# Gate and up weights of sixteen experts in one 16 KB-run transfer, down weights in 8 KB runs: one layer step on one Trainium2 core

## The chip, the cores and the metric

The kernel runs as one program on one core of a Trainium2 chip. Its time is the device time of one execution in microseconds (us); several executions are timed and the median is given. One further execution is profiled, which records every instruction, wait and DMA packet.

## The reference, cut to what matters

One decoder layer is computed for 1024 new prompt tokens and 8 sequences of 8 sampled tokens (1088 tokens of width 1024): a norm, one q/k/v projection, two kinds of attention (partly over cached pages), an output projection, and a mixture of 16 experts of which every token takes two. Only the experts matter here:

```python
# 4 groups x 4 experts; w_gate, w_up: (.., 1024, 256); w_down: (.., 256, 1024); all float32
a = silu(einsum('nd,gedf->ngef', xt, w_gate)) * einsum('nd,gedf->ngef', xt, w_up)
y = einsum('ngef,gefd->nd', a * gates[..., None], w_down)     # gates: two of 16 are not zero
x = x + y
```

Gate, up and down weights take 1 MB each for an expert, 3 MB in all.

## The kernel before

The stages run one after the other: projection, attention, output projection, `route`, `experts`. `route` (L2043) picks two experts for each token and sorts the tokens by expert into tiles of 128 rows: 32 tile slots (`MOE_TILES`), of which an expert fills as many as it needs. Which expert a tile belongs to is known only on the chip, so `tile_expert`, `tile_load` and `tile_place` are tables in memory that the engines read into registers (L2374, L2385, L2386).

`experts` (L2310) walks over the 32 tiles. For a tile the engines do this:

- SyncE (SP) issues the weight loads. Every tile has three transfers, each with a condition (`cond=load`): gate and up (L2395), down (L2400). A transfer whose condition is 0 moves nothing, but raises its semaphore like one that ran. A tile's expert is loaded only in the first tile of that expert. There are four places for weights (`W_PLACES`). The gate and up transfers of a tile wait until the tile four before it has been split (`gu_lo`); the down transfer waits until the down product of the tile four before is in PSUM (`y_done`). As the SP's queue goes in order, the next tile's gate and up transfers come right behind that wait. The weights of experts 0 and 1 are loaded ahead in `route` by `load_ahead` (L2028), with three transfers each and without a condition, and the SP waits for those of a tile before it goes on (L2389).
- ScalarE (ACT) and VectorE (DVE) split gate and up weights into a high and a low part (L2574, L2516), in two halves of 128 x 2048 elements. ACT's split waits for `gu_loaded` (L2567).
- TensorE (PE) multiplies the rows with the split weights, 24 matmuls (`gate_up`, L2467), turns the next tile's rows round (L2445), makes the down product of the tile before (`down`, L2489), and turns the activations round (L2476). Tile 0 is multiplied with whole weights, 16 matmuls (L2457).
- ACT and DVE copy the two halves of the down product out of PSUM (`keep_y`, L2605, L2539). Both wait for the addition two tiles back, since `expert_out` has two buffers.
- GpSimd (POOL) gathers the rows of the tile (L2038) and adds the result rows to the residual in memory with an indirect, accumulating DMA (L2423). Each addition waits until the one before it has landed. Gathers and additions go through the software DMA queue q0; all that SP issues goes through the hardware queue q1. Both run on the same 16 DMA engines.

A transfer from DRAM is moved as runs that are contiguous on both sides. Partition p of the gate weights holds rows 8p to 8p+7, each of 256 numbers: one run of 8 KB. Partition p of the down weights holds rows p and 128+p, each of 1024 numbers: two runs of 4 KB.

After the last addition the SP loads the residual rows back, they are normed, and stored.

Of the kernel before, what the change touches and what calls it, by code (L numbers as in the profile page):

```python
# [10 lines left out]
F32 = mybir.dt.float32  # L11
# [21 lines left out]
P = 128  # L33
# [1965 lines left out]
def expert_places(nc, ctx, t):  # L1999

    def keep(name, shape, dt=F32):
        return ctx.enter_context(nc.sbuf_tensor(name, shape, dt))

    t.slot_gate = keep("slot_gate", [P, MOE_TILES])
    t.slot_tok = keep("slot_tok", [P, MOE_TILES], I32)
    t.slot_out = keep("slot_out", [P, MOE_TILES], I32)
    t.adds_wanted = keep("adds_wanted", [1, 1], I32)
    t.tile_expert = keep("tile_expert", [1, MOE_TILES], I32)
    t.tile_load = keep("tile_load", [1, MOE_TILES], I32)
    t.tile_place = keep("tile_place", [1, MOE_TILES], I32)  # L2010
    t.w_gu = keep("w_gate_up", [P, W_PLACES, 2, KC, D_EXPERT])
    t.w_dn = keep("w_down", [P, W_PLACES, FK, D_MODEL])
    t.slot_rows = keep("slot_rows", [P, ROW_PLACES, D_MODEL])
    assert place_ahead(N_EXPERTS - 1) == 0
    freed = t.w_gu[:, 1:W_PLACES, :, :, :].rearrange("p a c k n -> p (a c k n)").rearrange("p (t n) -> p t n", n=D_MODEL)
    t.x1_rows, t.g_final_row, t.square3 = freed[:, 0:TILES, :], freed[:, TILES, :], freed[:, TILES + 1, :]
    t.x1_loaded = [ctx.enter_context(nc.semaphore(f"x1_loaded{n}")) for n in range(TILES)]
    t.g_final_loaded = ctx.enter_context(nc.semaphore("g_final_loaded"))
    t.w_ahead = [ctx.enter_context(nc.semaphore(f"expert_ahead{n}")) for n in range(W_AHEAD)]
    t.added = ctx.enter_context(nc.semaphore("expert_rows_added"))  # L2020
    t.rows_loaded = [ctx.enter_context(nc.semaphore(f"slot_rows_loaded{n}")) for n in range(ROW_PLACES)]
# [6 lines left out]
def load_ahead(engine, t, e):  # L2028


    n = place_ahead(e)
    for c, w in enumerate((t.w_gate, t.w_up)):
        engine.dma_start(t.w_gu[:, n, c, :, :], w[e].rearrange("(p k) n -> p k n", p=P)).then_inc(t.w_ahead[e], 16)
    engine.dma_start(t.w_dn[:, n, :, :], t.w_down[e].rearrange("(k p) n -> p k n", p=P)).then_inc(t.w_ahead[e], 16)

# [274 lines left out]
def experts(nc, t):  # L2310

    with ExitStack() as ctx:
# [67 lines left out]
        with nc.Block() as block:  # L2380

            @block.sync
            def _(sp):
                for tile in range(MOE_TILES):
                    e = sp.value_load(t.tile_expert[0:1, tile:tile + 1], min_val=0, max_val=N_EXPERTS - 1)  # L2385
                    load = sp.value_load(t.tile_load[0:1, tile:tile + 1], min_val=0, max_val=1)  # L2386
                    at = place(sp, tile)
                    if tile < W_AHEAD:
                        sp.wait_ge(t.w_ahead[tile], 48)  # L2389
                    gu_lo.reached(sp, tile - W_PLACES, 1)  # L2390
                    if tile == W_PLACES:
                        gu_done.reached(sp, 0)
                    own_wait(sp, t)
                    for n, w in enumerate((t.w_gate, t.w_up)):
                        sp.dma_start(w_gu[:, bass.ds(at, 1), n, :, :].rearrange("p a k n -> p (a k) n"),  # L2395
                                     w[bass.ds(e, 1), :, :].rearrange("e (p k) n -> p (e k) n", p=P),
                                     cond=load).then_inc(gu_loaded[tile % W_PLACES], 16)
                    y_done.reached(sp, tile - W_PLACES, 1)
                    own_wait(sp, t)
                    sp.dma_start(w_dn[:, bass.ds(at, 1), :, :].rearrange("p a k n -> p (a k) n"),  # L2400
                                 t.w_down[bass.ds(e, 1), :, :].rearrange("e (k p) n -> p (e k) n", p=P),
                                 cond=load).then_inc(dn_loaded[tile % W_PLACES], 16)
# [36 lines left out]
            def _(pe):  # L2439
# [10 lines left out]
                def gate_up(tile):  # L2450
                    u = tile % 2
                    if tile == 0:
                        pe.wait_ge(t.w_ahead[0], 48)
                        for k in range(KC):
                            if k % 4 == 0:
                                xT_hi.reached(pe, 0, k // 4)
                            last = pe.matmul(gu_ps[:, 0, :].rearrange("p (c n) -> p c n", c=2), whole_T[:, k, :],  # L2457
                                             w_gu[:, place_ahead(0), :, k, :], start=(k == 0), stop=(k == KC - 1))
                        last.then_inc(gu_done.sem, 1)
                        return  # L2460
# [18 lines left out]
                def down(tile, halves=(0, 1)):  # L2479
# [3 lines left out]
                    if tile < W_AHEAD:  # L2483
                        pe.wait_ge(t.w_ahead[tile], 48)
                    for c in halves:
# [22 lines left out]
            def _(dve):  # L2508
                def split_gu(tile):

                    raw = w_gu[:, bass.ds(place(dve, tile), 1), :, :, :].rearrange("p a c k n -> p k (a c) n")
                    for half in range(2):
                        at, u = slice(4 * half, 4 * half + 4), tile % 2
                        gu_hi.reached(dve, tile, half)
                        own_wait(dve, t)
                        dve.tensor_tensor(gu_split[:, u, 1, at, :].rearrange("p k (c n) -> p k c n", c=2), raw[:, at, :, :],  # L2516
                                          gu_split[:, u, 0, at, :].bitcast(F32).rearrange("p k (c n) -> p k c n", c=2),
                                          ALU.subtract).then_inc(gu_lo.sem, 1)
# [44 lines left out]
            def _(act):  # L2563
                def split_gu(tile):

                    raw = w_gu[:, bass.ds(place(act, tile), 1), :, :, :].rearrange("p a c k n -> p k (a c) n")
                    act.wait_ge(gu_loaded[tile % W_PLACES], 32 * (tile // W_PLACES) + 32)  # L2567
                    if tile < W_AHEAD:
                        act.wait_ge(t.w_ahead[tile], 48)
                    gu_done.reached(act, tile - 2)  # L2570
                    own_wait(act, t)
                    for half in range(2):
                        at, u = slice(4 * half, 4 * half + 4), tile % 2
                        act.activation(gu_split[:, u, 0, at, :].rearrange("p k (c n) -> p k c n", c=2), raw[:, at, :, :],  # L2574
                                       ACT.Copy).then_inc(gu_hi.sem, 1)

# [73 lines left out]
def host_constants():  # L2650
# [26 lines left out]
INPUTS = ["x", "cache_kT_d", "cache_v_d", "cache_kT_s", "cache_v_s", "page_table", "rel_bias", "g_mix", "w_in", "lambda_q1", "lambda_k1", "lambda_q2",  # L2677
          "lambda_k2", "subln_g", "w_out", "g_ffn", "w_group", "b_group", "w_erouter", "b_erouter", "w_gate", "w_up",
          "w_down", "g_final", "eye", "bucket_table", "mask_rows", "half_map", "rank_const", "column_const", "spare_const", "before_const", "token_const", "sum_map"]
# [96 lines left out]
```

## Time and profile before

| | |
|---|---|
| median of 3 timed executions | 1261.24 us (1259.09 to 1262.69) |
| the profiled execution, its own time | 1258.88 us |
| its span, first to last instruction | 1256.9 us |
| mean granted TensorE clock | 0.971 of full speed |
| PE busy in the span | 1156.9 us (92%) |
| DVE, ACT, POOL busy | 698.2, 597.1, 142.5 us |
| route and experts | from 875 us to the end |

The profile gives for each engine when it was busy, what ended each wait, and for each DMA queue how many packets and bytes moved in a stretch of time. 2 us of the profiled execution's time lie outside its span. The busy share of PE is an average over all stages; what the change is worth has to be read from the expert stage alone.

### The profile page before, as it was taken

Reading aid. Unit: us, or ns where it says so; the run is one execution under the profiler, and the core shown is the slowest. Engines: PE = TensorE matmul, PEld = TensorE weight load, DVE = VectorE, ACT = ScalarE, POOL = GpSimd, SP = SyncE. Lnnn points to the kernel's source line nnn. Section 1 sums busy time; section 2 is a strip of 40 time slices with the busy share of each in tenths; the row PEclk is TensorE's granted clock in tenths of the full one; section 3 lists DMA queues with packets and bytes.
Section 4 is the critical chain, followed back from the end, with each engine's and each line's share of the span. In section 5 each row is a group of like instructions: output and inputs, shape, how many; then the busy total and the mean of one; then the engine's idle time right before and its main releaser. Section 6 shows DMA issues by size and latency. Waiting matters only on the chain. (4 is left out here: it accounts for less than half of the span.)

```text
span 1256.9 us, 23325 instructions
## 1 busy us (share of the span) xinstructions
PE 1156.9 (92%) x7695; PEld 815.2 (65%) x7695; DVE 698.2 (56%) x1048; ACT 597.1 (48%) x1030; POOL 142.5 (11%) x172
## 2 busy tenths in 40 slices
PE   7999999999688999979999999997689999999992
PEld 5877888888445555544655567875367766667771
DVE  4322112220177776658899977444566666666664
ACT  5520122201176776737568554232155655556654
POOL 1100000000011111100000000000123222433311
PEclk9999999999899999989999999999689999999997
DMA  6642244317599999999999946442679999865476
GB/s 209 218 132 77 82 148 126 101 42 250 189 360 381 345 374 386 382 380 379 383 362 371 387 159 185 155 147 107 245 274 363 375 378 297 239 171 112 101 218 193
DMA packets 155392, 307.43 MB, mean 245 GB/s; under 512 B 22311, under 2 KB 49354, under 8 KB 151178
## 3 DMA queue, kind: packets, MB, share of 16 engines
q1 hardware_dynamic: 145018, 272.38, 60.0%
q0 software_dynamic: 9216, 33.56, 11.5%
q8 instruction: 64, 1.05, 0.3%
q14 instruction: 54, 0.44, 0.1%
q10 hardware_dynamic: 1040, 0.00, 0.0%
HBM read 308.31 MB, written 54.72 MB: 289 GB/s over the span
## 5 line engine op out<-in xcount | busy, mean ns | idle before, releaser
L327 PE MATMUL proj_ps<-w_in_split,x_T_hi 128*128 128x512 f32 x608 | 194.6, 395 | 2.7 <-DVE w_in_split L369 2.7
L2516 DVE TENSOR_TENSOR w_gate_up_split<-w_gate_up,w_gate_up_split 128x2048 fp32r<-128x2048 f32 x62 | 139.3, 2288 | 87.3 <-ACT w_gate_up_split L2574 87.3
L2467 PE MATMUL gate_up_ps<-w_gate_up_split,slot_rows_T 128*128 128x512 f32 x744 | 180.3, 398 | 2.1 <-DVE slot_rows_T L2524 1.9
L2467 PEld LDWEIGHTS gate_up_ps<-w_gate_up_split,slot_rows_T 128*128 128x128 f32 x744 | 139.2, 191 | 31.9 <-DVE slot_rows_T L2524 3.4
L327 PEld LDWEIGHTS proj_ps<-w_in_split,x_T_hi 128*128 128x128 f32 x608 | 115.0, 189 | 27.8 <-DVE x_T_lo L364 2.5
L455 ACT ACTIVATE proj_rows<-proj_ps,sum_squares 128x512 f32<-128x512 f32 x38 | 26.2, 689 | 211.9 <-PE proj_ps L327 200.3
L327 PE MATMUL proj_ps<-w_in_split,x_T_lo 128*128 128x512 f32 x304 | 119.1, 392 | 0.0
L2574 ACT ACTIVATE w_gate_up_split<-w_gate_up 128x2048 fp32r x62 | 115.3, 1912 | 6.7 <-DMA w_gate_up<-in_w_up 5.4
L2489 PE MATMUL expert_out_ps<-w_down,expert_act_T 128*128 x256 | 115.3, 593 | 0.3 <-issue 0.3
L1736 PE MATMUL mix_out_ps<-w_out_split,oT_split 128*128 128x512 f32 x420 | 101.2, 396 | 0.3 <-DVE w_out_split L1875 0.3
L1142 PE MATMUL turns_and_scores_ps<-head_kT,head_qT 64*128 64x512 f32 (+3 forms) x384 | 85.9, 537 | 16.2 <-DMA head_kT<-scratch_kT 9.9
L1736 PEld LDWEIGHTS mix_out_ps<-w_out_split,oT_split 128*128 128x128 f32 x420 | 77.6, 188 | 18.9 <-DVE w_out_split L1875 1.8
L1317 DVE TENSOR_TENSOR_SCAN rest_products<-rest_products 128x128 f32<-128x128 f32 (+7 forms) x64 | 84.2, 1342 | 3.4 <-ACT rest_products L1478 3.4
L322 PE MATMUL proj_ps<-x_T_hi,w_in_split 128*128 128x512 f32 x256 | 82.3, 396 | 0.0
L1506 ACT ACTIVATE weights_T<-turns_and_scores_ps 128x1024 f32<-128x1024 f32 (+6 forms) x80 | 58.8, 742 | 42.1 <-PE turns_and_scores_ps L1156 41.6
L2423 POOL DMA_INDIRECT scratch_x<-expert_out,slot_out x32 | 58.2, 1818 | 179.5 <-DMA scratch_x<-expert_out,slot_out 95.2
L2489 PEld LDWEIGHTS expert_out_ps<-w_down,expert_act_T 128*128 128x128 f32 x256 | 46.2, 190 | 46.5 <-issue 46.4
L1240 PE MATMUL sample_o_ps<-pages,sample_weights_T 128*32 128x256 f32 x1024 | 71.1, 385 | 0.4 <-ACT sample_weights_T L1557 0.4
L369 DVE SCALAR_TENSOR_TENSOR w_in_split<-w_in_now,g_mix_T,w_in_split 128x512 fp32r<-128x512 f32 x48 | 35.6, 748 | 58.8 <-ACT w_in_split L441 58.8
L1206 PE MATMUL turns_and_scores_ps<-pages,q_by_block 128*32 128x256 f32 x912 | 61.2, 391 | 5.1 <-ACT betas L1482 3.4
L327 PEld LDWEIGHTS proj_ps<-w_in_split,x_T_lo 128*128 128x128 f32 x304 | 57.6, 189 | 11.3
L1118 POOL TENSOR_SCALAR stats<-stats 128x1 f32<-128x1 f32 x32 | 8.9, 279 | 445.4 <-ACT o_squares L1516 445.4
(255 smaller groups left out, 1750.1 us busy)
## 6 DMA issues: line engine op xcount, KB each, us to landing
w_gate_up<-in_w_gate SPq DMA_DIRECT2D x34, 1024.0 KB, 8.4
w_gate_up<-in_w_up SPq DMA_DIRECT2D x34, 1024.0 KB, 10.2
w_down<-in_w_down SPq DMA_DIRECT2D x34, 1024.0 KB, 12.3
pages<-in_cache_v_d SPq DMA_DIRECT2D x128, 256.0 KB, 5.9
pages<-in_cache_kT_s SPq DMA_DIRECT2D x128, 256.0 KB, 5.7
pages<-in_cache_v_s SPq DMA_DIRECT2D x128, 256.0 KB, 6.0
pages<-in_cache_kT_d SPq DMA_DIRECT2D x100, 256.0 KB, 6.2
w_in_now<-in_w_in SPq DMA_DIRECT2D x48, 256.0 KB, 3.0
```

What stands on the lines that cost most here:

```text
L322: last = pe.matmul(pj_ps[:, n % PJ_BANKS, 0:c1 - c0], w[g % 2][:, k, at], h[:, k, c0:c1], start=(k == 0 and m == 0), stop=(k == KC - 1 and ...
L327: last = pe.matmul(pj_ps[:, n % PJ_BANKS, :], h[:, k, at], w[g % 2][:, k, :], start=(k == 0 and m == 0), stop=(k == KC - 1 and m == 2))
L1142: last = pe.matmul(ring[places["score", it, i, g]][:, u, 0:k1 - k0], qT[half(u), it % 2, i * P:(i + 1) * P], kT[half(u), it % 2, k0:k1], s ...
L1206: last = pe.matmul(out, q_block[:, e, b, :], keys, start=(part == 0), stop=(part == 1))
L1240: last = pe.matmul(sO_ps[rows, :], sT[0:n, s, rows], page_v[0:n, c // 2, b:b + 2, :], start=(s == 0), stop=(s == D_PAGES - 1))
L1317: dve.tensor_tensor_scan(x, x, x, 1.0, ALU.mult, ALU.bypass).then_inc(scans.sem, 1)
L1506: act.activation(wT[:, at:at + m, :], blocks_of("out", it, i, n)[:, 0:m, :], ACT.Copy)\
L1736: last = pe.matmul(y_ps[:, m % Y_BANKS, :], oT_split[:, n % 2, a, k, :], w_split[:, b, k, c * BANK:(c + 1) * BANK], start=(m > 0 and at == ...
L2467: last = pe.matmul(gu_ps[:, u, :], xT[:, u, a, k, :], gu_split[:, u, b, k, :], start=(k == 0 and m == 0), stop=(k == KC - 1 and m == 2))
L2489: last = pe.matmul(y_ps[:, c, :], aT[:, u, k, :], w_dn[:, bass.ds(at, 1), k, c * BANK:(c + 1) * BANK] .rearrange("p a n -> p (a n)"), star ...
L2516: dve.tensor_tensor(gu_split[:, u, 1, at, :].rearrange("p k (c n) -> p k c n", c=2), raw[:, at, :, :], gu_split[:, u, 0, at, :].bitcast(F3 ...
L2574: act.activation(gu_split[:, u, 0, at, :].rearrange("p k (c n) -> p k c n", c=2), raw[:, at, :, :], ACT.Copy).then_inc(gu_hi.sem, 1)
```

## The change

The host packs gate and up weights of an expert side by side (`w_gate_up`, 1024 rows of 512 numbers), and reorders the down weights so that partition p holds two neighbouring rows. In memory on the chip, the tile `w_gate_up` has the same size as before, with gate and up of one row of the weights side by side. So a transfer of gate and up is one of 2 MB with one contiguous run of 16 KB for each partition, in place of two of 1 MB with runs of 8 KB. The down transfer stays at 1 MB, with one run of 8 KB for each partition in place of two of 4 KB. The bytes are the same. Each tile has two conditional transfers in place of three, and an expert loaded ahead has two in place of three. The operands of the splits and of tile 0's matmuls become contiguous where they were two pieces of 256 for each k; their number and sizes stay. Counts that are waited for become smaller with the number of transfers.

```diff
-    t.w_gu = keep("w_gate_up", [P, W_PLACES, 2, KC, D_EXPERT])
+    t.w_gu = keep("w_gate_up", [P, W_PLACES, KC, GU])
...
-    for c, w in enumerate((t.w_gate, t.w_up)):
-        engine.dma_start(t.w_gu[:, n, c, :, :], w[e].rearrange("(p k) n -> p k n", p=P)).then_inc(t.w_ahead[e], 16)
-    engine.dma_start(t.w_dn[:, n, :, :], t.w_down[e].rearrange("(k p) n -> p k n", p=P)).then_inc(t.w_ahead[e], 16)
+    engine.dma_start(t.w_gu[:, n, :, :], t.w_gate_up[e].rearrange("(p k) n -> p k n", p=P)).then_inc(t.w_ahead[e], 16)
+    engine.dma_start(t.w_dn[:, n, :, :], t.w_down[e].rearrange("(p k) n -> p k n", p=P)).then_inc(t.w_ahead[e], 16)
...
-                        sp.wait_ge(t.w_ahead[tile], 48)
+                        sp.wait_ge(t.w_ahead[tile], 32)
...
-                    for n, w in enumerate((t.w_gate, t.w_up)):
-                        sp.dma_start(w_gu[:, bass.ds(at, 1), n, :, :].rearrange("p a k n -> p (a k) n"),
-                                     w[bass.ds(e, 1), :, :].rearrange("e (p k) n -> p (e k) n", p=P),
-                                     cond=load).then_inc(gu_loaded[tile % W_PLACES], 16)
+                    sp.dma_start(w_gu[:, bass.ds(at, 1), :, :].rearrange("p a k n -> p (a k) n"),
+                                 t.w_gate_up[bass.ds(e, 1), :, :].rearrange("e (p k) n -> p (e k) n", p=P),
+                                 cond=load).then_inc(gu_loaded[tile % W_PLACES], 16)
...
-                                 t.w_down[bass.ds(e, 1), :, :].rearrange("e (k p) n -> p (e k) n", p=P),
+                                 t.w_down[bass.ds(e, 1), :, :].rearrange("e (p k) n -> p (e k) n", p=P),
...
-                            last = pe.matmul(gu_ps[:, 0, :].rearrange("p (c n) -> p c n", c=2), whole_T[:, k, :],
-                                             w_gu[:, place_ahead(0), :, k, :], start=(k == 0), stop=(k == KC - 1))
+                            last = pe.matmul(gu_ps[:, 0, :], whole_T[:, k, :],
+                                             w_gu[:, place_ahead(0), k, :], start=(k == 0), stop=(k == KC - 1))
...
-                        dve.tensor_tensor(gu_split[:, u, 1, at, :].rearrange("p k (c n) -> p k c n", c=2), raw[:, at, :, :],
-                                          gu_split[:, u, 0, at, :].bitcast(F32).rearrange("p k (c n) -> p k c n", c=2),
+                        dve.tensor_tensor(gu_split[:, u, 1, at, :], raw[:, at, :], gu_split[:, u, 0, at, :].bitcast(F32),
                                           ALU.subtract).then_inc(gu_lo.sem, 1)
...
-                    act.wait_ge(gu_loaded[tile % W_PLACES], 32 * (tile // W_PLACES) + 32)
+                    act.wait_ge(gu_loaded[tile % W_PLACES], 16 * (tile // W_PLACES) + 16)
...
-                        act.activation(gu_split[:, u, 0, at, :].rearrange("p k (c n) -> p k c n", c=2), raw[:, at, :, :],
-                                       ACT.Copy).then_inc(gu_hi.sem, 1)
+                        act.activation(gu_split[:, u, 0, at, :], raw[:, at, :], ACT.Copy).then_inc(gu_hi.sem, 1)
...
-    for name in ("w_gate", "w_up"):
-        host[name] = a[name][0].reshape(N_EXPERTS, D_MODEL, D_EXPERT)
-    host["w_down"] = a["w_down"][0].reshape(N_EXPERTS, D_EXPERT, D_MODEL)
+    host["w_gate_up"] = np.concatenate([a[name][0].reshape(N_EXPERTS, D_MODEL, D_EXPERT) for name in ("w_gate", "w_up")], axis=2)
+    host["w_down"] = a["w_down"][0].reshape(N_EXPERTS, FK, P, D_MODEL).transpose(0, 2, 1, 3).reshape(N_EXPERTS, D_EXPERT, D_MODEL)
```

## Rows read from the trace of the kernel before

**Rows 1.** One window: busy us of PE, PEld, DVE, ACT, POOL, clock, DMA share, GB/s

```profile
1000.00:1050.00 50.00, 49.11 (x203) 33.52 (x201) 32.40 (x28) 28.65 (x33) 10.39 (x9) 1.00 1.03 371
```

**Rows 2.** Chain that ended last, start of the expert stage: start us, us, what

```profile
906.88 0.06 DMA w_gate_up<-in_w_up
...
907.15 1.92 ACT w_gate_up_split L2574
...
911.52 2.29 DVE w_gate_up_split L2516
...
915.39 8.31 PE gate_up_ps L2467 x24
...
928.23 5.49 PE gate_up_ps L2467 x24
```

**Rows 3.** SP's own queue in order of time: start us, us, transfer issued

```profile
902.86 0.00 SPq L2395 DMA_DIRECT2D w_gate_up<-in_w_gate  x1
903.59 0.01 SPq L2395 DMA_DIRECT2D w_gate_up<-in_w_up  x1
...
906.59 0.08 SPq L2395 DMA_DIRECT2D w_gate_up<-in_w_gate  x1
...
1018.38 0.39 SPq L2400 DMA_DIRECT2D w_down<-in_w_down  x1
1021.17 0.11 SPq L2395 DMA_DIRECT2D w_gate_up<-in_w_gate  x1
```

**Rows 4.** The same chain, later: additions, then TensorE again

```profile
938.57 0.68 ACT expert_out L2605
...
939.59 11.37 DMA scratch_x<-expert_out,slot_out
...
1042.07 10.03 DMA scratch_x<-expert_out,slot_out
...
1052.18 0.29 ACT expert_out L2605
...
1071.42 5.48 PE gate_up_ps L2467 x24
...
1221.62 5.49 PE gate_up_ps L2467 x24
```

**Rows 5.** Waits from 1000 to 1075 us: total us, times, longest

```profile
ACT expert_out L2605 <- DMA scratch_x<-expert_out,slot_out: 5.8, 4, 2.2
```

**Rows 6.** DMA queues in 952:954, 985:987, 991:994, 1028:1032, 1052:1057: packets, MB, share

```profile
q1 hardware_dynamic: 209, 0.86, 103.8%
...
q1 hardware_dynamic: 101, 0.41, 50.2%
q0 software_dynamic: 102, 0.41, 49.7%
...
q0 software_dynamic: 79, 0.32, 53.8%
q1 hardware_dynamic: 78, 0.61, 50.7%
...
q1 hardware_dynamic: 195, 0.83, 51.1%
...
q1 hardware_dynamic: 287, 1.12, 54.6%
```

**Rows 7.** All 32 additions (L2423), issue to landing

```profile
DMA to landing us min/median/max: 5.8/7.2/11.4
```

**Rows 8.** Groups of instructions: split halves and a four times smaller subtraction

```profile
L2516 DVE TENSOR_TENSOR w_gate_up_split<-w_gate_up,w_gate_up_split 128x2048 fp32r<-128x2048 f32 x62 | 139.3, 2288 | 87.3 <-ACT w_gate_up_split L2574 87.3
...
L2524 DVE TENSOR_TENSOR slot_rows_T<-slot_rows_T_ps,slot_rows_T 128x512 fp32r<-128x512 f32 x62 | 39.6, 680 | 0.2 <-ACT slot_rows_T L2583 0.2
```

**Rows 9.** Windows of 1 us, columns as in rows 1

```profile
914.00:915.00 1.00, 0.69 (x2) 0.29 (x2) 1.00 (x3) 0.08 (x1) 0.00 (x0) 0.53 0.94 365
...
920.00:921.00 1.00, 1.00 (x4) 0.78 (x3) 1.00 (x2) 0.00 (x0) 0.00 (x0) 0.55 0.99 406
```

More of the change, by code:

```diff
@@ L2014, in expert_places @@
     assert place_ahead(N_EXPERTS - 1) == 0
-    freed = t.w_gu[:, 1:W_PLACES, :, :, :].rearrange("p a c k n -> p (a c k n)").rearrange("p (t n) -> p t n", n=D_MODEL)
+    freed = t.w_gu[:, 1:W_PLACES, :, :].rearrange("p a k n -> p (a k n)").rearrange("p (t n) -> p t n", n=D_MODEL)
     t.x1_rows, t.g_final_row, t.square3 = freed[:, 0:TILES, :], freed[:, TILES, :], freed[:, TILES + 1, :]
@@ L2452, in gate_up @@
                     if tile == 0:
-                        pe.wait_ge(t.w_ahead[0], 48)
+                        pe.wait_ge(t.w_ahead[0], 32)
                         for k in range(KC):
@@ L2483, in down @@
                     if tile < W_AHEAD:
-                        pe.wait_ge(t.w_ahead[tile], 48)
+                        pe.wait_ge(t.w_ahead[tile], 32)
                     for c in halves:
@@ L2509, in split_gu @@
                 def split_gu(tile):
-                    raw = w_gu[:, bass.ds(place(dve, tile), 1), :, :, :].rearrange("p a c k n -> p k (a c) n")
+                    raw = w_gu[:, bass.ds(place(dve, tile), 1), :, :].rearrange("p a k n -> p (a k) n")
                     for half in range(2):
@@ L2564, in split_gu @@
                 def split_gu(tile):
-                    raw = w_gu[:, bass.ds(place(act, tile), 1), :, :, :].rearrange("p a c k n -> p k (a c) n")
-                    act.wait_ge(gu_loaded[tile % W_PLACES], 32 * (tile // W_PLACES) + 32)
+                    raw = w_gu[:, bass.ds(place(act, tile), 1), :, :].rearrange("p a k n -> p (a k) n")
+                    act.wait_ge(gu_loaded[tile % W_PLACES], 16 * (tile // W_PLACES) + 16)
                     if tile < W_AHEAD:
-                        act.wait_ge(t.w_ahead[tile], 48)
+                        act.wait_ge(t.w_ahead[tile], 32)
                     gu_done.reached(act, tile - 2)
@@ L2677 @@
 INPUTS = ["x", "cache_kT_d", "cache_v_d", "cache_kT_s", "cache_v_s", "page_table", "rel_bias", "g_mix", "w_in", "lambda_q1", "lambda_k1", "lambda_q2",
-          "lambda_k2", "subln_g", "w_out", "g_ffn", "w_group", "b_group", "w_erouter", "b_erouter", "w_gate", "w_up",
+          "lambda_k2", "subln_g", "w_out", "g_ffn", "w_group", "b_group", "w_erouter", "b_erouter", "w_gate_up",
           "w_down", "g_final", "eye", "bucket_table", "mask_rows", "half_map", "rank_const", "column_const", "spare_const", "before_const", "token_const", "sum_map"]
```

## The prediction

> **What bounds the kernel now.** I first read the page for the shares, and then only the expert stage, since the change touches nothing else. The window view shows PE busy for 49.11 of 50 us while the DMA engines are at a share of 1.03 [rows 1]: two resources are full at once. The chain that ended last says which one sets the end. It enters the stage through SP's queue: an SP transfer ends a wait, ACT splits tile 1's weights, DVE subtracts and copies rows, and PE starts tile 1 at 915.39 [rows 2]. From 928.23 on a tile should take (1221.62 - 1071.42) / 15 = 10.01 us, the pace of an unstalled PE [rows 4]. From 928.23 to 1071.42 lie 14 tiles, 140.2 us at that pace, but 143.2 us passed [rows 2, 4]. So PE loses 3.0 us to waits in the stretch in which weights are loaded, and nothing after it. The chain says to whom: it runs through additions, the first issued at 939.59, the last at 1042.07 [rows 4]. These are ten, each of which waits for the one before; from 939.59 to the landing of the last, 1052.10, they take 11.25 us each against PE's 10.01. ACT's copy of the down product waits for them four times, 5.8 us together, 2.2 at the longest [rows 5]. An addition lands 5.8 us after its issue at the least and 11.4 us at the most [rows 7]: the weight loads make it late.
>
> The packets show how. In 952:954 q1 alone moves 0.43 MB/us, in packets of 4.1 KB. In 985:987 both queues are busy and move 101 and 102 packets, all of 4 KB. In 991:994 they move 78 and 79, but those of q1 have 8 KB: 0.61 MB against 0.32 [rows 6]. The engines take one packet from one queue, then one from the other, whatever its length. The packet is the contiguous run, and the run is what the change doubles.
>
> **The change part by part.**
>
> *One conditional transfer fewer, start of the stage.* ACT's split of tile 1 starts 0.27 us after SP's up transfer of tile 1 at 906.88 [rows 2]. That transfer moves nothing (expert 1 was loaded ahead), but its semaphore ends the wait; so SP's queue is the path. On it lie tile 0's gate and up transfers, 903.59 - 902.86 = 0.73 us apart, and tile 1's, 906.88 - 906.59 = 0.29 us apart [rows 2, 3]. One of each goes: 1.0 us. All that follows to 915.39 (ACT, DVE, DVE) is work without slack, so tile 1 starts 1.0 us earlier, and with it SP's loads and the first addition. The bounds: 0.3 us, if the 0.73 is a stall that moves to the next transfer, and 1.3 us. I take 1.0. In the steady stage SP waits for `y_done` for most of a tile, and its removed transfer is worth nothing: that wait hides it. Without that cover it would be 0.3 to 0.7 us a tile.
>
> *The splits and tile 0's matmuls.* Their operands become contiguous. The subtraction takes 2288 ns for 2048 elements in four times two pieces, a smaller one 680 ns for 512: 1608 / 1536 = 1.05 ns an element and 0.14 us at the start, with nothing left for the pieces [rows 8]. Nothing gained, between 0 and the 0.14 us of one start a half, hidden by PE.
>
> *Load bytes and rates.* The bytes stay. 4 KB packets alone already run at 0.43 MB/us (0.86 MB in 2 us) [rows 6]. The nearest figure for longer ones is the mixed window's 0.61 MB in 1.5 us of q1's share, 0.40. I take no gain and no loss. The bounds: at 0.40 in place of 0.43 an expert's 3.1 MB take 0.5 us more, 5 us of engine time over ten experts; in the other direction, no more than PE's 3.0 us of stall can vanish.
>
> *The run length in front of the additions.* Of an addition's 128 rows each of 16 engines moves 8, one packet each. With gate and up runs queued, each waits for one of q1's packets: 8 KB at 0.43 MB/us over 16 engines is 0.31 us, 16 KB is 0.61 us. Eight of them cost 2.4 us more for each addition. Against down runs it is 8 x (0.31 - 0.15) = 1.2 us more. But q1 can go ahead only with what is queued. In 1028:1032 it still moves 4 KB runs, that is down weights issued at 1018.38, with gate and up of 1021.17 behind them [rows 3, 6]: up to 3 MB, 7 us of loads, could pass an addition there. At the last critical addition, landing at 1052.10, what q1 has left is the 1.12 MB of 1052:1057, 2.6 us [rows 6]. So an addition around 1030 gets later by 0 to 7 us, the one at 1052.10 by 0 to 2.6. What is served early is not served later, so the additions catch up. PE's stall follows the addition that is latest against PE's pace. The copy that waits for the one at 1052.10 comes 11 tiles after the copy at 938.57 [rows 4], so at 10.01 us a tile it is due at 1048.7: 3.4 us behind. The addition two before (about 1030, due 1028.7) is 1.3 behind. With 2.0 us more at the last it is 5.4 behind; with 4 us more at 1030 that one is 5.3 behind, which comes to the same. I take 2.0, near the upper end of 2.6, since in the nearest row, the one of 8 KB, double length did take double bytes. So the stall grows by +2.0; bounds 0 and +5 (7 us more at 1030, 8.3 behind in place of 3.4).
>
> *The other rule.* The Trainium skill (DMA: Bandwidth & Descriptors, Queues, rings and completion order) says that an engine drains a whole packet, typically 9 to 17 descriptors, from one ring before it switches. The rows show one recorded packet against one. By that rule the additions would wait for 9 to 17 runs at each switch and not for one: 8 x 9 x 0.31 us, 22 us an addition before the change, where the longest landing is 11.4 in all. So its packet isn't a row's packet here, and the sum goes by the row.
>
> **Sum.** -1.0 + 0 + 0 + 2.0 = +1.0 us on the profiled execution: its span 1256.9 and the 2.0 around it, 1258.88, become 1259.9. The median of the runs shown, 1261.24, lies 2.4 above it; the same difference gives 1262.2.
>
> **The rivals.**
>
> *The clock stays up.* PE stands still before tile 1, and its granted clock is 0.53 of full in 914:915 and 0.55 in 920:921, the low level (1.2 GHz) from about 914.1 to 920.9 [rows 9]. Tile 1's 24 matmuls take 8.31 us, tile 2's 5.49 [rows 2]: the low level costs 2.8 us. PE's next work came in the same window (busy 0.69 us of it). With work there 1.0 us sooner the clock may not fall: 1262.2 - 2.8 = 1259.4. Against it: most of the standstill stays.
>
> *Run length doesn't matter.* If the new transfer is cut into the same packets as before, or the queue holds too little to pass the additions, only the first part remains: 1261.2 - 1.0 = 1260.2. For it: the rows show no packet above 8 KB. Against: both lengths there are one run each.
>
> *Additions become the bound (the other side).* Before, an addition lands 10.0 us after its issue under load [rows 4] and 5.8 without [rows 7]: q1 is in front of it for 4.2 of the 7.3 us that an expert's 3.1 MB take at 0.43 MB/us, and the rest passes in the addition's idle parts (descriptors made, end signalled). With longer runs q1 empties its queue in front of the addition, and then the engines stand idle in those parts. If it is 5.0 us in place of 4.2, ten additions get 8 us later, and no catching up follows, since the loads are paced by PE, which waits as well: +8 - 1 = +7, 1268. It decides once q1 runs dry between additions. For it: the doubled bytes in 991:994. Against: nine tiles in a row load an expert each, so that the queue is long.
>
> *Faster engines.* The 3.0 us of stall vanish with the 1.0: 1257.2, or less with the clock.
>
> **How the numbers follow.** Forecast 0.35 (its own range 1259.5 to 1265), clock up 0.2, run length without effect 0.15, additions as the bound 0.22, faster engines 0.08. A measurement of this kernel tells a change from none at about 0.3%, 3.8 us: 1257.5 and 1265.0. Faster: the 0.08 and half of the clock case, which reaches below 1257.5 where the additions don't get later, 0.18. Slower: 0.22 and the forecast's tail, 0.25. Within: 0.57. The range 1257 to 1268 leaves out about 0.1 on each side.
>
> **What would show it.** SP's first transfer for tile 1 at about 905.9 and PE's tile 1 at 914.4. Packets of 16 KB in q1, one against one of q0, with 0.1 MB of q0 for 0.4 of q1. Additions that land 11 to 13 us after issue from 975 to 1030, in place of 10 to 11, and then catch up; ACT's waits for them at 8 us in place of 5.8; gate and up weights landing earlier. I am wrong if q1's packets stay at 8 KB, if additions land no later, or if tile 1's matmuls run at the full clock.

## The result

| | before | after | ratio, 95% interval |
|---|---|---|---|
| median of 15 timed executions each, side by side | 1260.4 us | 1266.69 us | 1.0049 [1.0038, 1.0059] |
| the same, once more (28 and 12 executions) | 1260.38 us | 1264.79 us | 1.0040 [1.0026, 1.0054] |
| span of the profiled execution | 1256.9 us | 1265.2 us | |

The changed kernel is slower, by 4 to 6 us. The forecast was 1262.2, with 1257 to 1268 as the range. So the range holds the result, but the estimate is 4.5 us short: 1266.7 lies above the 1259.5 to 1265 that the forecast had as its own range, in the part that the prediction called slower (0.25), and nearest to the rival of 1268. The second comparison, 4.4 us above the kernel before, is at the upper edge of the forecast's own range.

The start of the stage in the chain that ended last, after the change (start us, us, what):

```profile
909.46 0.06 DMA w_gate_up<-in_w_gate_up
...
909.74 1.92 ACT w_gate_up_split L2571
...
914.10 2.28 DVE w_gate_up_split L2514
```

It is the path of [rows 2], step by step, with SP's single transfer where its second one was. Before the 8.3 us of longer span are put down to the change, it has to be seen where the stage begins. Below is the router's first operation in DVE's timeline: of before, of after, and of a second profile of each (experiments e8 and e9 below):

```profile
875.04 0.19 DVE L2134 TENSOR_REDUCE g_max<-logits 128x9 f32<-128x36 f32 x1 [0.32 <-PEq L1669]
```
```profile
879.06 0.19 DVE L2133 TENSOR_REDUCE g_max<-logits 128x9 f32<-128x36 f32 x1 [0.32 <-PEq L1669]
```
```profile
878.82 0.19 DVE L2134 TENSOR_REDUCE g_max<-logits 128x9 f32<-128x36 f32 x1 [0.33 <-PEq L1669]
```
```profile
875.64 0.19 DVE L2133 TENSOR_REDUCE g_max<-logits 128x9 f32<-128x36 f32 x1 [0.33 <-PEq L1669]
```

Each kernel has an early and a late one. So 4.0 of the 8.3 us belong to the execution and not to the change, and from here on everything is counted from this operation. It leaves 1256.9 - 875.04 = 381.9 us before and 1265.2 - 879.06 = 386.1 us after.

This is tile 1 in TensorE's timeline, of after and of the second profile of before:

```profile
917.97 7.25 PE L2465 MATMUL gate_up_ps<-w_gate_up_split,slot_rows_T 128*128 128x512 f32 x24 [0.75 <-DVE slot_rows_T L2521]
```
```profile
918.02 5.78 PE L2467 MATMUL gate_up_ps<-w_gate_up_split,slot_rows_T 128*128 128x512 f32 x24 [0.76 <-DVE slot_rows_T L2524]
```

And its clock after, two windows of 1 us with the columns of [rows 1]:

```profile
914.00:915.00 1.00, 0.89 (x9) 0.66 (x6) 1.00 (x2) 0.99 (x2) 0.00 (x0) 1.00 0.00 0
...
918.00:919.00 1.00, 1.00 (x3) 0.81 (x4) 0.00 (x0) 1.00 (x1) 0.00 (x0) 0.50 1.11 475
```

The granted clock is full at 914, and at the low level (0.50, 1.2 GHz) at 918, after PE had stood still for most of 915 to 918. Compared with [rows 9], the clock still falls, but stays low for a shorter time (3.4 us against 6.8).

Then the additions, further on in the chain that ended last:

```profile
990.97 11.96 DMA scratch_x<-expert_out,slot_out
...
1003.72 12.52 DMA scratch_x<-expert_out,slot_out
...
1017.03 12.35 DMA scratch_x<-expert_out,slot_out
...
1029.46 0.30 ACT expert_out L2601
...
1038.44 5.78 PE gate_up_ps L2465 x24
...
1229.80 5.49 PE gate_up_ps L2465 x24
```

The additions of the same numbers before the change, in its chain:

```profile
986.27 10.25 DMA scratch_x<-expert_out,slot_out
...
997.31 10.19 DMA scratch_x<-expert_out,slot_out
...
1008.29 10.82 DMA scratch_x<-expert_out,slot_out
```

Three in a row take 12.0 to 12.5 us in place of 10.2 to 10.8. The last of them lands at 1029.38 against 1019.11, though the addition with the number of the first one in [rows 4] had started only 1.9 us later than before (941.5 against 939.6). While this lasts, PE starts a tile every 12.4, 13.3 and 13.1 us (999.6, 1012.0, 1025.3, 1038.4). PE's lost time is counted from the start of tile 2, 929.50, to that of the last tile, 29 tiles later, at 1229.55, which is 300.05 us. At the unstalled pace (150.20 / 15 = 10.013 us a tile) it would be 290.4, so 9.7 us are lost, against 3.0 before. The waits from 985 to 1075 us, to be compared with [rows 5]:

```profile
DVE expert_out L2536 <- DMA scratch_x<-expert_out,slot_out: 15.2, 5, 4.4
ACT expert_out L2601 <- DMA scratch_x<-expert_out,slot_out: 13.4, 4, 4.7
```

ACT's 5.8 us have become 13.4. The queues after, in 985:987, 1012:1014 and 1042:1054:

```profile
q1 hardware_dynamic: 52, 0.43, 52.6%
q0 software_dynamic: 50, 0.20, 49.1%
...
q1 hardware_dynamic: 36, 0.59, 70.3%
q0 software_dynamic: 32, 0.13, 32.7%
...
q0 software_dynamic: 525, 1.95, 79.1%
q1 hardware_dynamic: 6, 0.02, 0.5%
```

In the first window q1's packets have 8 KB (the down weights now, which were the 4 KB of [rows 6]), in the second 16 KB, and they alternate with q0's nearly one for one. What passes an addition between its issue and its landing has grown with it. These are q1's packets and bytes in that time, for one addition before (1008.29:1019.11) and for two after (1003.72:1016.24 and 1017.03:1029.38):

```profile
q1 hardware_dynamic: 525, 3.00, 67.6%
...
q1 hardware_dynamic: 354, 3.71, 70.5%
...
q1 hardware_dynamic: 338, 3.55, 68.4%
```

Before, it is about the 3.1 MB of one expert; after, it is 0.6 to 0.7 MB more, 1.3 to 1.7 us at the 0.43 MB/us of [rows 6].

From 1042 to 1054, q1 moves next to nothing. The weights are not done by then: another expert's 3.15 MB come from 1054 to 1068. But SP may issue them only when PE has finished the down product of an earlier tile, and PE is late. These are q1 in 1054:1068, and SP's wait in 1010:1060:

```profile
q1 hardware_dynamic: 288, 3.15, 60.9%
```
```profile
SPq L86 <- PE expert_out_ps L2487: 34.5, 4, 10.2
```

Last, the windows of both resources after, columns as in [rows 1]:

```profile
980.00:1005.00 25.00, 25.00 (x108) 18.14 (x107) 13.94 (x13) 14.49 (x17) 4.82 (x4) 1.00 1.02 380
1005.00:1030.00 25.00, 20.26 (x83) 13.36 (x82) 13.32 (x12) 10.67 (x14) 3.83 (x4) 1.00 1.03 383
1030.00:1042.00 12.00, 9.35 (x38) 6.00 (x37) 7.00 (x7) 7.82 (x9) 4.13 (x3) 1.00 0.96 354
1042.00:1054.00 12.00, 12.00 (x52) 8.61 (x51) 8.99 (x8) 8.12 (x9) 3.54 (x3) 1.00 0.80 166
```

The DMA engines are full (1.03) just where PE misses 4.7 of 25 us. They do not work less, they work in another order: from 940 to 1042 q1 moves 28.29 MB after and 27.63 MB before, although tile 2 began 1.5 us later. The weights were ahead, and the additions paid for it.

### The profile page after: what moved, and what is told of

Read it like the earlier page. It is cut to its first block and busy times, and to the rows that moved or that the text cites. A ratio compares the mean times of both kernels' runs of the same rounds, so it can differ in the third digit from the quotient of the medians.

```text
span 1265.2 us, 23259 instructions
## 1 busy us (share of the span) xinstructions
PE 1156.3 (91%) x7695; PEld 814.2 (64%) x7695; DVE 698.4 (55%) x1048; ACT 597.8 (47%) x1030; POOL 149.1 (12%) x172
## 3 DMA queue, kind: packets, MB, share of 16 engines
q1 hardware_dynamic: 140666, 272.38, 59.7%
q0 software_dynamic: 9216, 33.56, 11.5%
## 5 line engine op out<-in xcount | busy, mean ns | idle before, releaser
L2514 DVE TENSOR_TENSOR w_gate_up_split<-w_gate_up,w_gate_up_split 128x2048 fp32r<-128x2048 f32 x62 | 139.3, 2288 | 86.6 <-ACT w_gate_up_split L2571 86.6
L1142 PE MATMUL turns_and_scores_ps<-head_kT,head_qT 64*128 64x512 f32 (+3 forms) x384 | 85.8, 537 | 20.4 <-DMA head_kT<-scratch_kT 10.1
L2421 POOL DMA_INDIRECT scratch_x<-expert_out,slot_out x32 | 65.8, 2056 | 189.4 <-DMA scratch_x<-expert_out,slot_out 95.9
L327 PEld LDWEIGHTS proj_ps<-w_in_split,x_T_lo 128*128 128x128 f32 x304 | 57.6, 189 | 11.3
```

What stands on the lines that cost most here:

```text
L327: last = pe.matmul(pj_ps[:, n % PJ_BANKS, :], h[:, k, at], w[g % 2][:, k, :], start=(k == 0 and m == 0), stop=(k == KC - 1 and m == 2))
L1142: last = pe.matmul(ring[places["score", it, i, g]][:, u, 0:k1 - k0], qT[half(u), it % 2, i * P:(i + 1) * P], kT[half(u), it % 2, k0:k1], s ...
L2421: pool.indirect_dma_start(t.x1[:, :], bass.IndirectOffsetOnAxis(ap=t.slot_out[:, tile:tile + 1], axis=0), y[:, tile % 2, :], None, compute ...
L2514: dve.tensor_tensor(gu_split[:, u, 1, at, :], raw[:, at, :], gu_split[:, u, 0, at, :].bitcast(F32), ALU.subtract).then_inc(gu_lo.sem, 1)
```

## The experiments

All but e8, which is one profile, are timed beside the kernel before on the same chip. "Places for y" is the number of buffers for the down product. "Lost" is PE's lost time as above; "start" is from the router's first operation to tile 1.

| | gate and up | down | places for y | ratio, 95% interval | lost us | start us | tile 1 us |
|---|---|---|---|---|---|---|---|
| before, first profile | 2 transfers, 8 KB | 4 KB | 2 | 1 | 3.0 | 40.35 | 8.31 |
| e8, before again | 2 transfers, 8 KB | 4 KB | 2 | | 3.8 | 39.20 | 5.78 |
| after | 1, 16 KB | 8 KB | 2 | 1.0049 [1.0038, 1.0059] | 9.7 | 38.91 | 7.25 |
| e9, after again | 1, 16 KB | 8 KB | 2 | 1.0040 [1.0026, 1.0054] | 9.3 | 38.67 | 7.33 |
| e1 | 1, 16 KB | 4 KB | 2 | 1.0001 [0.9988, 1.0015] | 5.5 | 38.85 | 5.75 |
| e2 | 2, 8 KB | 8 KB | 2 | 1.002 [1.0004, 1.0035] | 4.2 | 39.29 | 8.62 |
| e3 | 1, two of 8 KB | 4 KB | 2 | 0.9986 [0.9973, 0.9998] | 4.9 | 38.86 | 5.75 |
| e4 | 1, four of 4 KB | 4 KB | 2 | 1.0017 [1.0003, 1.003] | 5.3 | 38.88 | 5.74 |
| e5 | 1, 16 KB | 8 KB | 3 | 0.9998 [0.9986, 1.0011] | 0.7 | 38.73 | 7.21 |
| e6 | 2, 8 KB | 4 KB | 3 | 0.9991 [0.9976, 1.0006] | 2.8 | 39.23 | 7.06 |
| e7 | 1, two of 8 KB | 4 KB | 3 | 0.998 [0.9966, 0.9994] | 3.1 | 38.83 | 5.74 |
| e11, e7 again | 1, two of 8 KB | 4 KB | 3 | 0.9983 [0.9967, 0.9998] | 4.0 | 38.94 | 5.74 |
| e10 | 1, 16 KB | 4 KB | 3 | 0.9969 [0.9955, 0.9982] | 0.1 | 38.78 | 5.76 |

**e1: the changed kernel with down weights in 4 KB runs again.**

```diff
-    engine.dma_start(t.w_dn[:, n, :, :], t.w_down[e].rearrange("(p k) n -> p k n", p=P)).then_inc(t.w_ahead[e], 16)
+    engine.dma_start(t.w_dn[:, n, :, :], t.w_down[e].rearrange("(k p) n -> p k n", p=P)).then_inc(t.w_ahead[e], 16)
```

(and the same in SP's conditional transfer and on the host)

> Gate and up as in the change (one transfer, runs of 16 KB), down weights with 4 KB runs as before. Theory (each packet of the weight queue goes in front of one packet of an addition, so run length sets how late additions land): additions against gate and up wait as in the changed kernel, additions against down weights as before, so most of the loss stays: 1.002 to 1.005 of before; additions land 11 to 12.5 us after issue between 980 and 1040 us. Rival (the loss comes from the down weights, or from something outside the expert stage): 0.998 to 1.001.

1261.67 us beside 1261.43. I had expected most of the loss to stay, since 16 KB runs are the longer ones, and it is gone. Its queues in 1005:1007 and 1012:1014:

```profile
q0 software_dynamic: 67, 0.27, 68.5%
q1 hardware_dynamic: 62, 0.25, 33.1%
...
q1 hardware_dynamic: 55, 0.84, 99.0%
q0 software_dynamic: 1, 0.00, 0.0%
```

In the first window an addition passes and meets the down weights, 4 KB against 4 KB. In the second the 16 KB runs have the engines for themselves, since q0 is between two of its transfers. This is not a matter of one window. Below are e1's addition before this one, in 1001:1004 (q1 alone, 16 KB) and 1004:1010, and the changed kernel in 1009:1014:

```profile
q1 hardware_dynamic: 83, 1.31, 101.6%
...
q0 software_dynamic: 220, 0.84, 56.3%
q1 hardware_dynamic: 221, 1.05, 44.0%
...
q1 hardware_dynamic: 94, 1.49, 71.2%
q0 software_dynamic: 85, 0.35, 34.7%
```

An addition gets late by what it meets. In e1 the additions around here meet mostly the short runs and land 10.4 to 11.0 us after issue; in the changed kernel they meet the long ones and land after 12.0 to 12.5.

**e2: the kernel before, with down weights in 8 KB runs.** The same edit the other way.

> Gate and up as before (two transfers, 8 KB runs), only the down weights with 8 KB runs. Theory: 1.2 us more for an addition that meets down weights, none for one that meets gate and up, and no gain at the start: 1.000 to 1.003 of before. Rival (run length doesn't matter): 1.000.

1263.56 us, 1.002. The ratio is as expected, the reason is not: the seven additions issued from 979 to 1046 land after 10.1 to 10.8 us, before after 9.7 to 10.8, so the expected 1.2 us more are not there. PE loses 4.2 us against 3.0 and 3.8, and tile 1 took 8.62 us in this profile. So 8 KB down runs alone are worth about +2 us, of which the profile gives 0.4 to 1.2 to waits after tile 2, and neither half of the change alone makes the whole loss. Together they do: e1 less e3, 16 KB in place of 8 KB, is +0.0015, e2 less before +0.002, both together less e3 +0.0054 to 0.0063. With intervals of 0.0013 to each side of a ratio that alone would not be firm, but the lost times say it too: 3.0 and 3.8 before, 4.2 and 5.5 with one of them, 9.7 and 9.3 with both. With both lengths doubled there is no short run left for an addition to meet.

**e3: one transfer for gate and up, in two runs of 8 KB for each partition; down 4 KB.** The change without its longer runs; the edit is against the changed kernel.

```diff
+GU_RUNS = 2
...
-                    sp.dma_start(w_gu[:, bass.ds(at, 1), :, :].rearrange("p a k n -> p (a k) n"),
-                                 t.w_gate_up[bass.ds(e, 1), :, :].rearrange("e (p k) n -> p (e k) n", p=P),
+                    sp.dma_start(w_gu[:, bass.ds(at, 1), :, :].rearrange("p a (h k) n -> p (a h) (k n)", h=GU_RUNS),
+                                 t.w_gate_up[bass.ds(e, 1), :, :].rearrange("e (h p k) n -> p (e h) (k n)", h=GU_RUNS, p=P),
```

> One transfer for gate and up, but the host lays the weights out so that each partition gets two runs of 8 KB; down weights with 4 KB runs as before. So only the number of transfers differs from before. Theory: tile 1 starts 1.0 to 1.6 us earlier and additions land as before: 0.998 to 0.9995. Rival (the packing itself, or one large transfer, is what makes it slower): 1.003 or more.

1259.31 us, 0.9986. The merged transfer, the side by side layout and the contiguous operands cost nothing; if anything they give 2 us. The ratio is in the expected range, though the start gained 0.3 to 0.4 us on e8 and e2 and not 1.0 to 1.6. The loss is in the run lengths.

**e4: the same with four runs of 4 KB (`GU_RUNS = 4`).**

> As the run before this one, but four runs of 4 KB a partition for gate and up. Theory: an addition waits for 4 KB where it waited for 8, 8 x 0.15 = 1.2 us less for each against gate and up; additions land after 9 us, TensorE's stall of 3.0 us goes, and the start gains 1.0 to 1.6: 0.996 to 0.998. Rival (short runs are slower to move, weights come late): 1.000 or more, with ACT's split waiting for weights.

1263.13 us, 1.0017, where 0.996 to 0.998 was expected: the rival's way. The additions are earlier, 9.1 to 10.8 us from 985 to 1049, and ACT and DVE don't wait for one from 985 to 1075. But ACT waits for gate and up weights there, and the chain runs through one of these transfers:

```profile
ACT w_gate_up_split L2573 <- DMA w_gate_up<-in_w_gate_up: 10.4, 5, 2.9
```
```profile
1020.16 23.53 DMA w_gate_up<-in_w_gate_up
```

So the run length moves the wait from one queue to the other: 4 KB makes the weights late, 16 and 8 KB together the additions, and the 8 and 4 KB of before lie between the two.

**e5: the changed kernel with three places for the down product.** Gate and activations share one buffer, which makes the room. The lengths of all runs and the work stay.

```diff
-                    if tile >= 2:
-                        act.wait_ge(t.added, 16 * (tile - 1))
-                    act.activation(y[:, u, 0:BANK], y_ps[:, 0, :], ACT.Copy, scale=t.slot_gate[:, tile:tile + 1])\
+                    if tile >= Y_PLACES:
+                        act.wait_ge(t.added, 16 * (tile - Y_PLACES + 1))
+                    act.activation(y[:, tile % Y_PLACES, 0:BANK], y_ps[:, 0, :], ACT.Copy, scale=t.slot_gate[:, tile:tile + 1])\
```

(with `Y_PLACES = 3`; the same in DVE's half and in the addition; `silu_gate` has one place, is multiplied in place, and ACT waits for `aT_done` of the tile before)

> The changed kernel with three buffers for the expert outputs in place of two, so that ACT and VectorE copy a down product without waiting for the addition two tiles back, but three back (room comes from one buffer for the activations in place of four). Theory (TensorE's 9.7 us of lost time come from additions that land late): the third buffer gives each addition 10 us more, so 7 to 9.7 us of them go: 0.996 to 0.999 of the kernel before the change. Rival (weights or another wait is behind it): no gain, 1.004.

1258.94 us beside 1259.76; the changed kernel has 1266.69 and 1264.79 beside 1260.4. The additions issued from 979 to 1026 land after 10.3 to 13.0 us, two of the five after more than 11, but from 985 to 1075 only POOL waits for one:

```profile
POOL scratch_x L2421 <- DMA scratch_x<-expert_out,slot_out: 53.5, 7, 10.4
```

PE's loss falls from 9.7 to 0.7 us. This is the most direct evidence for the cause: with the same run lengths, and ACT and DVE no longer behind the additions, PE does not stall. The time fell less than the loss, by 5 to 7 us against 9, so that 0.9998 lies just above what was expected (0.996 to 0.999); where the rest went is not shown.

**e6: the kernel before with three places.**

> The kernel before the change with the same three buffers. Theory: its 3.0 us of lost time go, 0.997 to 0.998 of the kernel before. Rival (with the additions out of the way the weights come late, as they are at the edge too): 0.998 to 1.001.

1259.8 us, 0.9991: level with before, as the rival had it (0.998 to 1.001). The waits for additions are gone here too, and in their place ACT waits for weights, 940 to 1130 us:

```profile
ACT w_gate_up_split L2573 <- DMA w_gate_up<-in_w_up: 5.8, 3, 2.8
```

With one limit taken away, PE still loses 2.8 us to the other, against 3.0 and 3.8 with both: the two limits of the kernel before lie side by side.

**e7: e3 with three places.**

> One transfer for gate and up with two runs of 8 KB a partition, down weights with 4 KB runs, and three buffers for the expert outputs. Theory: the start gains 1.5 us and up to 2.6 from a clock that stays up at tile 1, and the 4.9 us that TensorE lost in the same kernel with two buffers go: 0.993 to 0.996. Rival (the weights are the next bound): 0.996 to 0.999, with ACT's split waiting for weights.

1257.36 us, 0.998, where 0.993 to 0.996 was expected; again the rival. Weights are the limit as in e6 (5.2 us of ACT's wait, longest 2.9), and PE loses 3.1 us.

**e8: the kernel before, one more profile.**

> The kernel before, unchanged, profiled once more: where does its expert stage begin, and at which clock does tile 1 run? If the 4 us by which the changed kernel's expert stage begins later are a matter of the single execution, it begins at 875 to 880 us here, where all others do; if the change causes them, at 875.

One timed execution, 1260.03 us. Tile 1 took 5.78 us in place of 8.31, and came 39.20 us after the router's first operation in place of 40.35. So both the clock step and 1.1 us of the start differ between executions of the same kernel.

**e9: the changed kernel again.**

> The changed kernel itself, unaltered, timed again beside the kernel before and profiled a second time. If the loss comes of longer runs in front of the additions, as the first seven runs made it, the ratio is again 1.003 to 1.006, the last ten or so additions under load land 11 to 13 us after issue, and PE loses 8 to 11 us between tile 2 and the last one (9.7 in the first profile). If a good part of the first profile's loss was that execution's own, the second profile shows 4 to 7 us and the ratio falls to 1.002 or less. Tile 1's 24 matmuls may take either 5.7 or 7.3 to 8.6 us: that clock step goes both ways between executions.

1.0040, lost 9.3 us, and the four additions issued from 974 to 1013 land after 11.5, 11.3, 12.9 and 12.1 us. It repeats, as expected. Its stage begins where that of [rows 2] does (875.64 against 875.04), and its span is 1261.5, 4.6 above. One thing is new: PE's standstill in front of a late tile let the clock fall as well. PE was busy for 0.13 us in 1018:1020, and the granted clock is low from 1020.4 to 1027. These are the tile's matmuls in PE's timeline, and the clock in 1022:1023:

```profile
1021.06 8.53 PE L2465 MATMUL gate_up_ps<-w_gate_up_split,slot_rows_T 128*128 128x512 f32 x24 [0.74 <-DVE slot_rows_T L2521]
```
```profile
1022.00:1023.00 1.00, 1.00 (x4) 0.72 (x3) 0.00 (x0) 0.00 (x0) 0.00 (x0) 0.50 1.08 332
```

They took 2.8 us more than the 5.75 of the tile before (1007.40). The chain that ended last runs through the next addition there (1025.67, landing at 1035.65), so this profile shows no cost of it at the end.

**e10: 16 KB for gate and up, 4 KB for down, three places (e1 with e5's edit); e11: e7 beside it.**

> The changed kernel's 16 KB gate and up runs with 4 KB down runs, and three places for the down product in place of two, so that ACT and DVE no longer wait for the addition before last (gate and activations share one buffer to make room). Theory: of the losses left in this stage one is late additions, taken away by the third place, and the other is late gate and up weights, which 8 KB runs leave at the edge (5.2 us of ACT's wait); 16 KB runs win the engines from the additions and bring the weights 1 to 3 us earlier, so that PE loses 0 to 2 us and the time is 0 to 3 us under that of the 8 KB version with three places, a ratio to the kernel before of 0.995 to 0.998. Rival: one packet against one, but with the additions no longer limiting them, the weights are paced by PE anyway; then the two are level, 0.997 to 0.9995.

> The version with one transfer of two 8 KB runs for gate and up, 4 KB down runs and three places for the down product, unaltered from its first run (0.998 [0.9966, 0.9994]). It is timed again so as to stand beside the 16 KB version on one chip. Expected 0.9965 to 0.9995; PE loses 2 to 4 us; if the 16 KB version is faster by weights that come earlier, this one is 1 to 3 us above it, and if run length no longer matters once the additions hold nobody up, they agree within 1 us.

e10 has 1256.63 us, 0.9969, and e11 1258.07 us, 0.9983, where before has 1260.38. Both are in their expected ranges. The intervals of the two overlap, so their times alone don't tell them apart; the profiles show the difference that the theory named. e10's wait for weights from 940 to 1130, and PE in two windows:

```profile
ACT w_gate_up_split L2570 <- DMA w_gate_up<-in_w_gate_up: 0.5, 1, 0.5
```
```profile
980.00:1040.00 60.00, 60.00 (x254) 42.08 (x253) 40.58 (x37) 36.27 (x43) 17.30 (x11) 1.00 1.03 378
1040.00:1100.00 60.00, 60.00 (x253) 42.13 (x252) 40.59 (x37) 36.44 (x42) 22.91 (x14) 1.00 0.90 268
```

In e11 ACT waits 6.2 us for weights there. In e10 PE loses 0.1 us in 29 tiles, in e7 and e11 3.1 and 4.0: once nothing waits for the additions, long gate and up runs take PE's loss away. It is the fastest version measured, 3.8 us under the kernel before.

## Why the prediction was right, and where it was short

**What bounds the kernel** held in part: two full resources, and before and after the change the chain runs through additions. But e6 shows that the weights stand right beside them, since PE loses 2.8 us when nothing waits for an addition. The engines' time says why. By [rows 6] an addition's row of 4 KB holds an engine for 0.327 us (79 packets, 53.8% of 16 engines in 3 us), a gathered row or a plain 4 KB run for 0.16 (102 and 101 packets, 49.7% and 50.2% in 2 us). So a tile with a new expert needs about 3.15 / 0.43 = 7.3 us for its weights, 128 x 0.327 / 16 = 2.6 for its addition and 1.3 for its gather: an estimate of 11.2 us, where PE needs 10.01. It agrees with the 11.25 us that the prediction measured between additions. In this stretch the engines can't keep up with PE, and the order of their work decides who is late.

**Start, -1.0.** Too large. From SP's first conditional transfer to the one that releases ACT (tile 0's to tile 1's last of gate and up) it is 906.88 - 902.86 = 4.02 us in [rows 2, 3], 3.24 in e8 (906.27 to 909.51), 2.86 after (906.60 to 909.46) and 2.84 in e9. So the change gives 0.4 us; the 0.73 between tile 0's two transfers was that execution's own (0.33 in e8), a case that the lower bound of 0.3 had named. By "start", before has 40.35 once and 39.2 to 39.3 three times (e2, e6, e8), one transfer fewer 38.7 to 38.9: 0.3 to 0.6 us. The expected places (SP's transfer for tile 1 at 905.9, tile 1 at 914.4) are met by e9 (905.80 and 914.31) by luck: its router began 0.60 us later than that of [rows 2], and the start it is compared with was a slow one.

**Splits at nothing** held: 2288 ns and 680 ns, the numbers of [rows 8], did not move. **Load rates at nothing** held: q1 moves 272.38 MB in both and has 60.0% and 59.7% of the engines; 0.84 MB of 16 KB runs in 2 us is the 0.43 MB/us of [rows 6] within 3%.

**Run length in front of the additions, +2.0.** The mechanism was right and this term was mis-sized: PE's loss went from 3.0 and 3.8 us to 9.7 and 9.3, +6.1 on the mean, where I took +2.0 and a bound of +5. The delay of one addition was near its estimate (1.5 to 2.3 us later, between the 1.2 of down runs and the 2.4 of gate and up). Both estimates came true only together, though: 16 KB gate and up runs alone (e1) and 8 KB down runs alone (e2) left the additions at 10.1 to 11.0 us. What failed is the step after it, which counted what is still queued at the last critical addition, 2.6 us at 1052, and let the additions catch up. The stall's peak moved forward: it is set by the landing at 1029.38, whose copy at PE's pace was due at 1018.7, plus the 1.5 us by which tile 2 itself was later, 1020.2. It came 9.2 us after that. In the kernel before, the addition of that number (landing 1019.11) was 0.4 us late. Four additions in a row each took 1.5 to 2.3 us longer than theirs of before. I had given the one that landed at about 1030 only +4 of a possible 7, in place of adding up those in front of it; it landed 9.5 us later (1039.6 against 1030.1), or 8.0 without the 1.5. And "what is served early is not served later" came true only after 1042, when q1 had run empty and additions landed in 6.4 us: too late, for PE had lost its time by then, and its loads had been held back with it. The range held by its width, which the rival of 1268 had given it, and not by this sum.

**The rivals.** "Additions become the bound" named the time, 1268 against 1266.7, and its picture of PE going at their pace is what 999.6 to 1038.4 shows, 12 to 13 us a tile. Its other part, that no catching up follows because the loads are paced by PE, is what q1's pause from 1042 shows. But its condition, that q1 runs dry between additions and the engines stand idle, is not what came: their share is 1.03 in that stretch, and q1 is dry only after it. So it was the forecast's exchange, order against order, at the rival's size.

"The clock stays up" did not come in either profile of the changed kernel, but tile 1 took 5.74 to 5.78 us in 7 of the 13 profiles and 7.06 to 8.62 in the others, once each way for the kernel before. Two patterns stand behind it. In the seven, the granted clock was 0.50 until 31.4 to 31.5 us after the router's first operation, tile 0's 16 matmuls took 9.2 to 9.3 us, and the clock then stayed full. In the six, it was full already from 28.2 to 28.8 us on, tile 0 took 7.7 to 8.0, PE stood still for longer before tile 1, and the clock fell at 38.4 to 39.0. All four profiles with 8 KB down runs are of the second kind, all six with one transfer and 4 KB down runs of the first. So part of the changed kernel's loss, about 1.5 us, may be the clock at tile 1. Over the timed executions, too, the mean granted clock is 0.9695 in both series of the changed kernel, 0.9703 in e2 and 0.9710 in e5, against 0.9711 to 0.9713 for the kernel before. 0.0018 of 1265 us is 2.3 us of full clock, an estimate of what the clock could make of the loss. A cause from the run length to the clock is not shown: it was not tested, and chance can't be excluded. PE's lost time is counted from tile 2 on and holds nothing of tile 1.

"Run length doesn't matter" and "faster engines" fell, by e3 and by the rates. The rule of the Trainium skill that was weighed (DMA: Bandwidth & Descriptors, Queues, rings and completion order), a drain of 9 to 17 descriptors before a switch, is not seen in the recorded packets with longer runs either: 52 against 50 and 36 against 32, and in 1009:1014 16 to 19 of q0 in each microsecond, about one for each of the 16 engines. The prediction's 22 us were no sound argument against it, though. By that rule the 8 runs that an engine moves of an addition would themselves pass in one turn, so there would be one switch and not eight, an estimate of 9 to 17 x 0.31 = 2.8 to 5.3 us, which the landings don't exclude. It is the packet counts that speak.

**The sum, again, in measured terms.** From the router's first operation on, profile after against profile before: start -1.4, clock at tile 1 and what lies to tile 2 -1.1 (12.6 against 11.5 us), PE's loss +6.7, the end +0.1: +4.3, where 386.1 - 381.9 is 4.2. Without what differs between executions: -0.4 + 6.1 = +5.7 us, where the two timed comparisons have +6.3 and +4.4. The clock at tile 1 is left out of this as open.

What stays open: that the additions of e1 meet short runs and those of the changed kernel don't was read from windows, and why the two fall so is not shown; no run shifted one against the other. That the two lengths do more together than the sum of each rests on ratios whose intervals are as wide as half the effect, and on one or two profiles of each.

## What to carry to other kernels

A longer run in one DMA queue takes engine time from every other queue that the engines serve in turn with it; before it is lengthened, look for who waits on the other queue, and give that one a buffer more first (16 and 8 KB runs with two places +0.4 to 0.5%, 16 and 4 KB with three -0.3%: 8.2 us between them on one chip). A delay that repeats adds up over a chain of dependent transfers as long as the load lasts, so its place is the row where the sum peaks, not the last critical one of before. And a stall of under 1 us in a single profile is weak ground for a term: a second profile of the same kernel moved the start by 1.1 us and tile 1's matmuls by 2.5.

## What the runs showed of the hardware that was not expected

- One packet against one from two queues holds for runs of 4, 8 and 16 KB (50 to 52 and 32 to 36 in the windows above): the share of bytes follows the run length, 0.59 MB against 0.13 at 16 KB to 4 KB.
- A 4 KB row of an accumulating DMA holds an engine as long as about 8 KB of a plain load: 0.327 us (32 packets, 32.7% of 16 engines in 1012:1014), where plain runs of 4, 8 and 16 KB hold it for 0.16, 0.31 and 0.62 ([rows 6] and the same window).
- The additions and the loads fall into step. In e1, e2 and e3, with runs of 16 and 4, 8 and 8, and 8 and 4 KB, seven or eight additions in a row land after 10.1 to 11.0 us, and q1 moves 2.9 to 3.1 MB between issue and landing (e1 at 999.4 and 1010.7, e2 at 1001.3, e3 at 997.2): one expert's weights for each addition, whatever the runs. In the changed kernel, with 16 and 8 KB, 3.6 to 3.8 MB pass, and three in a row take 12.0 to 12.5. Why the step holds in the first three and breaks in the last was not tested.
- A conditional transfer that moves nothing costs SP about 0.3 us (0.29 and 0.33 apart), and one fewer of each kind gave 0.4 us at the start, not the 1.0 of one profile.
